# TensorE's first products of an expert placed behind the chain of comparisons, with a hinted jump to the rest

## The chip, the cores and the metric

The kernel runs on one core of one Trainium2 chip. The metric is the device time of one launch in microseconds (us), a median of runs. TensorE does the matrix products (in the profile PE for the products and PEld for the loading of their weights), VectorE is DVE, ScalarE is ACT, GpSimd is POOL, and SyncE (SP) issues the large transfers.

## What is computed

Two layers of an encoder trunk over 256 tokens of width 1024. The second layer ends in a mixture of experts, and the change touches that part alone:

```python
def moe_swiglu(h, w_router, b_router, w_gate_e, w_up_e, w_down_e):
    t = h.reshape(n, d)                                   # n = 256, d = 1024
    logits = (t @ w_router).astype(jnp.float32) + b_router.astype(jnp.float32)
    top_val, top_idx = lax.top_k(logits, TOP_K)           # 2 of 8 experts
    gates = jax.nn.softmax(top_val, axis=-1)
    ...
    def expert_block(args):
        xblk, e = args
        return swiglu(xblk, w_gate_e[e], w_up_e[e], w_down_e[e])   # width 3584
    ...
def swiglu(u, wg, wu, wd):
    return (jax.nn.silu(u @ wg) * (u @ wu)) @ wd
```

With the inputs of the measurement the eight experts get 3, 8, 109, 33, 131, 7, 166 and 55 rows.

## The kernel before

Every engine runs its own instruction stream. The experts are a loop over `turn` = 0 to 7 that each engine runs for itself. The routine `experts` (from line 668) writes it: the part `next` adds one to the counter and leaves after eight, `pick` loads the number of rows of this expert from `cnt`, and `tree` is a chain of compare-and-branch instructions that picks the body for 32, 64, 128, 160, 192 or 256 rows, the smallest that holds the count. So the bodies that run, in order, are those for **32, 32, 128, 64, 160, 32, 192 and 64** rows; this text calls them expert 0 to expert 7.

The bodies are written out in full, one behind the other, and are long on TensorE. An fp32 product (`mm` on F32 operands) is four instructions there, two weight loads and two matmuls, and an fp32r product is two. Counted in the built program, from the first instruction of `tree`, the bodies begin at 17 (128 rows), 1170 (32), 3531 (64), 4826 (160) and 7506 (192), and the last jump of the 160 body stands at 7504. A body begins with a hint (BRANCH_PREFETCH_HINT, written by `mark_branch_hint_location`) that names its own last instruction, a jump to `next`. The body for `first_variant`, 128 rows, stands straight behind `tree`. ScalarE and VectorE have the same structure with bodies of their own, and the change leaves theirs as they are.

An expert has 14 stages. A stage multiplies the rows by 256 columns of the gate and of the up weights (`gate_up`), applies silu and the product on ACT and DVE, turns the result (`turn`) and multiplies it by the down weights (`down`). Its weights are three units of 1 MB. SP fetches the units in order into 14 slots; a slot is free again when the stage that read it has counted up `gu_full` or `down_done`. For up to 64 rows `expert_whole` works on fp32 weights as they land. For 128 rows `expert_split`, for 160 and 192 rows `expert_wide`, ACT and DVE first split each unit into two fp32r parts (`conv_hi`, `conv_lo`); in `expert_wide` only stage 0 (`gate_up_whole`) uses the fp32 weights as they are, in two halves `h` of 16 products each. `xe_ready` says that the rows of the next expert have been copied by POOL.

[...]

## Time and profile before

| | us |
|---|---|
| median of three runs | 1688.39 |
| lowest and highest run | 1682.43, 1692.14 |
| the profiled execution | 1681.41 |
| its span, first to last instruction | 1679.6 |
| TensorE busy in the span | 1476.7 (88%) |
| the eight experts, from the first product of expert 0 | 680 to 1653 |

The profile says when each engine worked, what ended each idle stretch, and what the DMA queues moved. The windows list for each stretch the busy time and count of PE, PEld, DVE, ACT and POOL, then the granted share of TensorE's clock, the mean busy share of the DMA engines and what they moved.
### The profile page before, as it was taken

How to read it: one execution, taken by the hardware profiler on the slowest of the kernel's cores; microseconds unless marked ns; L12 is line 12 of the kernel's file. 1: busy time of each engine (PE TensorE's matmuls, PEld its weight loads, DVE VectorE, ACT ScalarE, POOL GpSimd, SP SyncE). 2: the span in 40 equal slices, each digit the busy share in tenths (PEclk: the TensorE clock that was granted, in tenths of full speed). 3: DMA queues.
4: the chain of work that ended last, by engine and by line, in shares of the span. 5: the costliest groups of instructions: out<-in, count | busy, mean ns of one | idle time of the engine just before them, and what ended most of it. 6: DMA issues, size and time to landing. Idle time of an engine off the chain costs nothing.

```text
span 1679.6 us, 30643 instructions
## 1 busy us (share of the span) xinstructions
PE 1476.7 (88%) x12410; PEld 1188.3 (71%) x12411; DVE 786.5 (47%) x1098; ACT 596.8 (36%) x795; POOL 69.4 (4%) x66
## 2 busy tenths in 40 slices
PE   5999899999999998765659999989996679999894
PEld 3878778999977876543548875689985468888452
DVE  2584565565556655100038851166761036665112
ACT  2445254444343433100036750146551035554101
POOL 0010100000010111000000000000000000000002
PEclk8999999999999999978789999999998889999998
DMA  9644567745333529899999999996667996555893
GB/s 361 238 159 172 202 225 293 282 176 197 141 116 109 223 76 386 352 425 423 425 425 426 406 384 425 424 391 279 244 270 312 425 424 249 224 226 225 329 425 148
DMA packets 69183, 488.89 MB, mean 291 GB/s; under 512 B 7744, under 2 KB 7776, under 8 KB 11168
## 3 DMA queue, kind: packets, MB, share of 16 engines
q1 hardware_dynamic: 66800, 479.94, 71.0%
q10 hardware_dynamic: 1648, 4.59, 0.8%
q8 instruction: 117, 1.92, 0.5%
q0 software_dynamic: 576, 2.10, 0.4%
q14 instruction: 42, 0.34, 0.1%
HBM read 482.66 MB, written 3.93 MB: 290 GB/s over the span
## 4 chain that ended last, share of the span: by engine, by line
PE 44%; DMA 10%; issue 4%; DVE 2%; ACT 1%; SPq 1%; POOL 1%; ACTq 0%; POOLq 0%; DVEq 0%
PE PG L1442 9%; DMA ring<-in_experts 8%; PE PG L1564 5%; PE PG L1499 4%; PE Y L1527 4%; PE Y L1454 4%; PE TRB L1499 4%; PE TRB L1505 3%; PE PG L1505 3%; PE Y L1595 2%; PE Y L1518 2%; DMA arena<-in_experts 2%; PE TRB L1428 2%; SPq L785 1%; PE Y L1251 1%
## 5 line engine op out<-in xcount | busy, mean ns | idle before, releaser
L2537 DVE COPY arena<-TRB 128x64 f32<-128x64 f32 (+1 forms) x70 | 17.6, 252 | 342.9 <-PE TRB L1428 342.9
L1442 PE MATMUL PG<-ring,mixT 128*32 128x128 f32 (+1 forms) x1920 | 115.3, 346 | 64.5 <-issue 59.9
L1647 ACT ACTIVATE rope<-PG 64x128 f32<-64x128 f32 (+2 forms) x84 | 27.3, 324 | 379.2 <-PE PG L1442 355.7
L1647 ACT ACTIVATE parts<-ring 128x2048 fp32r<-128x2048 f32 x82 | 153.7, 1902 | 9.4 <-PE PG L1564 5.1
L1442 PEld LDWEIGHTS PG<-ring,mixT 128*32 128x32 f32 (+1 forms) x1920 | 88.5, 137 | 94.5 <-issue 79.1
L944 PE MATMUL PG<-h_parts,parts 128*128 128x512 f32 x432 | 152.9, 394 | 1.4 <-DVE arena L2415 1.4
L1442 PE MATMUL PG<-arena,mixT 128*32 128x128 f32 (+1 forms) x1664 | 102.6, 355 | 41.8 <-issue 41.8
L1442 PEld LDWEIGHTS PG<-arena,mixT 128*32 128x32 f32 (+1 forms) x1664 | 79.7, 141 | 69.3 <-issue 55.7
L946 PE MATMUL PG<-h_parts,parts 128*128 128x256 f32 x432 | 121.8, 282 | 0.0
L2400 DVE TENSOR_TENSOR parts<-ring,parts 128x2048 fp32r<-128x2048 f32 x42 | 95.1, 2289 | 30.4 <-ACT parts L1647 30.4
L2521 DVE TENSOR_TENSOR ring_parts<-ring,parts 128x2048 fp32r<-128x2048 f32 x40 | 90.6, 2288 | 30.1 <-PE Y L1518 18.1
L2521 DVE TENSOR_TENSOR parts<-arena,parts 128x2048 fp32r<-128x2048 f32 x42 | 95.2, 2288 | 17.5 <-PE Y L1518 13.5
L944 PEld LDWEIGHTS PG<-h_parts,parts 128*128 128x128 f32 x432 | 81.2, 188 | 19.8 <-DVE arena L2415 1.6
L946 PEld LDWEIGHTS PG<-h_parts,parts 128*128 128x128 f32 x432 | 81.3, 188 | 0.0
L1647 ACT ACTIVATE parts<-arena 128x2048 fp32r<-128x2048 f32 x42 | 78.9, 1902 | 3.7 <-PE PG L1564 3.7
L911 PE MATMUL Y<-parts 128*128 128x256 f32 x224 | 63.5, 284 | 0.2 <-DVE parts L2424 0.2
L913 PE MATMUL Y<-parts 128*128 128x256 f32 x224 | 63.4, 283 | 0.0
L912 PE MATMUL Y<-parts 128*128 128x256 f32 x224 | 63.4, 283 | 0.0
L2090 DVE TENSOR_TENSOR ring_parts<-ring,ring_parts 128x2048 fp32r<-128x2048 f32 (+1 forms) x24 | 52.8, 2199 | 18.9 <-ACT ring_parts L1647 18.8
L2521 DVE TENSOR_TENSOR parts<-arena,scr_parts 128x2048 fp32r<-128x2048 f32 x21 | 48.2, 2293 | 26.4 <-ACT scr_parts L1647 26.4
L1454 PE MATMUL Y<-arena 128*32 128x256 f32 (+1 forms) x512 | 56.9, 445 | 3.0 <-issue 2.8
L1647 ACT ACTIVATE ring_parts<-ring 128x2048 fp32r<-128x2048 f32 (+1 forms) x24 | 43.8, 1837 | 41.3 <-PE Y L1251 30.1
(381 smaller groups left out, 2853.4 us busy)
## 6 DMA issues: line engine op xcount, KB each, us to landing
ring<-in_experts SPq DMA_DIRECT2D x168, 1024.0 KB, 14.0
arena<-in_experts SPq DMA_DIRECT2D x168, 1024.0 KB, 16.8
ring<-in_weights SPq DMA_DIRECT2D x116, 1024.0 KB, 6.5
ring<-in_weights SPq DMA_DIRECT2D x4, 512.0 KB, 5.2
ypairs<-hT ACTq DMA_DIRECT2D x3, 512.0 KB, 6.9
tok<-in_x SPq DMA_DIRECT2D x1, 1024.0 KB, 9.1
result<-scr SPq DMA_DIRECT2D x2, 512.0 KB, 2.6
ring<-in_weights SPq DMA_DIRECT2D x2, 432.0 KB, 6.0
```

The source lines that it names most:

```text
L911: mm(out_, w_hi[w][:, c], x[0], start=first, stop=False, skip_group_check=True)
L944: mm(PG[:, m, :].rearrange("p (i t) -> p i t", i=2), w_hi[d % SPLITS][:, c], h_parts[:, :, k, :], start=(k == 0), stop=False, skip_group_c ...
L946: last = mm(PG[:, m, 0:T], w_lo[d % SPLITS][:, c], h_hi[:, k, :], start=False, stop=(k == KD - 1), skip_group_check=True)
L1442: last = mm(bank[i * n:(i + 1) * n, 0:width], xe[:, k, 0:n], w[k // 4][:, k % 4, i * width:(i + 1) * width], start=(k == 0), stop=(k == KD ...
L1454: last = mm(o, actT[:, s % 2, f, 0:n], w[:, f, c:c + width], start=(s == 0 and f == 0), stop=(s == STAGES - 1 and f == 1))
L1499: last = mm(both, hi[:, k, i // 2, i % 2, :], h_parts[:, :, h * KD // 2 + k, 0:n], start=(h == 0 and k == 0), stop=False, skip_group_check ...
L1505: last = mm(bank[:, 0:n], lo[:, k, i // 2, i % 2, :], h_parts[:, 0, h * KD // 2 + k, 0:n], start=False, stop=(h == 1 and k == KD // 2 - 1) ...
L1527: last = mm(o, a[:, s % 2, f, :], w[:, f, c:c + width], start=(opens and s == 0 and f == 0), stop=(closes and s == STAGES - 1 and f == 1))
L1564: last = mm(bank, x[j][:, h * KD // 2 + k, :], w[:, k, :], start=(opens and k == 0), stop=(closes and k == KD // 2 - 1))
L1647: return nc.scalar.activation(out_, in_, func, **kw)
L2400: V.tensor_tensor(w_lo[d % SPLITS], ring[:, slot_of[slot_of_dense(d)], :, :].rearrange("p k c -> p (k c)"), w_hi[d % SPLITS].bitcast(F32), ...
L2521: V.tensor_tensor(w_lo_e[q % SLOTS_E], ring_e[q % SLOTS_E].rearrange("p k c -> p (k c)"), w_hi_e[q % HI].bitcast(F32), ALU.subtract).then_ ...
```

## The change

`experts` gets a parameter `heads`, which TensorE alone passes. For 64, 192 and 160 rows (`HEADS`) there is now a short body that stands straight behind `tree`: the wait for `xe_ready`, stage 0 of `gate_up` for 64 rows, or the first half of `gate_up_whole` for 160 and 192 rows, then a hinted jump to `rest_64`, `rest_192` or `rest_160`, which holds everything else. The body for 32 rows follows the heads and is whole. The bodies for 128 and 256 rows stay whole and stand farther back. The order of the products within an expert is the same as before.

```diff
+HEADS = (64, 192, 160)
...
-            for n in sorted(NVAR, key=lambda n: n != first_variant):
-                with nc.body(label(n), valid_engines=own):
+            if heads:
+                for n in HEADS:
+                    with nc.body(label(n), valid_engines=own):
+                        on = eng.mark_branch_hint_location()
+                        heads(eng.snap(turn, min_val=0, max_val=NE - 1), n)
+                        eng.br(label(f"rest_{n}")).branch_hint(on)
+            for n in sorted(NVAR, key=lambda n: n != (32 if heads else first_variant)):
+                parted = heads and n in HEADS
+                with nc.body(label(f"rest_{n}" if parted else n), valid_engines=own):
                     back = eng.mark_branch_hint_location()
+                    if heads and not parted:
+                        heads(eng.snap(turn, min_val=0, max_val=NE - 1), n)
                     emit(eng.snap(turn, min_val=0, max_val=NE - 1), n)
                     eng.br(label("next")).branch_hint(back)
...
-            def expert_whole(e, n):
+            def expert_whole(e, n, head):
...
-                for i in range(STAGES + 2):
+                if head:
+                    gate_up(0)
+                    return
+                for i in range(1, STAGES + 2):
...
-                gate_up_whole()
+                if head:
+                    gate_up_whole(0)
+                    return
+                gate_up_whole(1)
...
+                if head:
+                    gate_up(0)
+                    return
                 for s in range(STAGES + 1):
-                    if s < STAGES:
+                    if 0 < s < STAGES:
                         gate_up(s)
...
-            def expert(e, n):
+            def part(e, n, head):
+                (expert_whole if n < P else expert_split if n % P == 0 else expert_wide)(e, n, head)
+
+            def expert_head(e, n):
                 pe.wait_ge(xe_ready, e + 1)
-                (expert_whole if n < P else expert_split if n % P == 0 else expert_wide)(e, n)
-
-            experts(pe, "pe", expert)
+                part(e, n, True)
+
+            def expert_rest(e, n):
+                part(e, n, False)
+
+            experts(pe, "pe", expert_rest, first_variant=HEADS[0], heads=expert_head)
```

On TensorE this is what stands behind the load of the row count before the change. L691 and L693 are the comparisons, and L1564 belongs to the body for 128 rows:

```order
L684 UNCONDITIONAL_BRANCH
L691 COMPARE_AND_BRANCH x2
L693 COMPARE_AND_BRANCH x3
L696 BRANCH_PREFETCH_HINT
L697 ISA
L1468 ISA
L1580 ISA
L1564 MATMUL PG<-scr_parts,h_parts 128x512 x4
```

And this stands there in the changed kernel, whose lines are ten or more higher. L698 is a head's hint, L1452 are products of `gate_up` for 64 rows, L1495 those of `gate_up_whole`:

```order
L692 COMPARE_AND_BRANCH
L694 COMPARE_AND_BRANCH x4
L698 BRANCH_PREFETCH_HINT
L699 ISA
L1424 ISA
L1452 MATMUL PG<-ring,mixT 64x256 x16
L700 UNCONDITIONAL_BRANCH
...
L1495 MATMUL PG<-mixT,ring 128x160 x8
L1495 MATMUL TRB<-mixT,ring 128x160 x8
L700 UNCONDITIONAL_BRANCH
L704 BRANCH_PREFETCH_HINT
L706 ISA
L1424 ISA
L1452 MATMUL PG<-ring,mixT 32x128 x32
```

The 128 body has given its place to three heads of 16 products each (64 matmul and load instructions each), and the 32 body follows them. Counted from the first instruction of `tree` as before, the heads begin at 17, 87 and 156, the 32 body at 225, `rest_64` at 2587, the 128 body at 3816, `rest_160` at 4969 and `rest_192` at 7584.

The second place is the end of the 160 body on TensorE, before the change:

```order
L1468 REGISTER_ALU
L1535 REGISTER_ALU
L1527 MATMUL Y<-parts 128x512 x4
L1527 MATMUL Y<-parts,arow_parts 128x512 x4
L1527 MATMUL Y<-parts 128x512 x4
L698 UNCONDITIONAL_BRANCH
L696 BRANCH_PREFETCH_HINT
```

These products are the same in the changed kernel. What moved is the place of their jump in the stream: 7504 instructions behind `tree` before, 7582 now.

## Rows read from the trace of the kernel before

**Rows 1.** Page, part 4, chain that ended last: shares by engine.

```profile
PE 44%; DMA 10%; issue 4%; DVE 2%; ACT 1%; SPq 1%; POOL 1%; ACTq 0%; POOLq 0%; DVEq 0%
```

**Rows 2.** Windows: stretch, length, busy times, then PEclk, DMA share, GB/s.

```profile
758.00:864.00 106.00, 62.65 (x1165) 47.79 (x1156) 8.12 (x30) 5.80 (x17) 1.90 (x1) 0.81 1.01 424
871.00:997.00 126.00, 122.19 (x530) 98.83 (x531) 103.42 (x70) 86.44 (x71) 2.42 (x1) 0.97 1.00 411
998.00:1082.00 84.00, 83.13 (x616) 46.30 (x612) 10.77 (x29) 7.15 (x16) 1.90 (x1) 1.00 1.01 417
1082.00:1262.00 180.00, 173.67 (x1292) 155.74 (x1288) 118.83 (x100) 97.83 (x97) 1.90 (x1) 0.99 0.75 304
...
1567.00:1650.00 83.00, 83.00 (x606) 46.86 (x608) 10.08 (x28) 6.56 (x15) 0.00 (x0) 0.98 0.87 359
...
1268.00:1276.00 8.00, 3.94 (x76) 3.96 (x80) 0.00 (x0) 0.19 (x1) 0.00 (x0) 0.50 0.12 36
1300.00:1340.00 40.00, 26.22 (x480) 19.76 (x484) 2.60 (x10) 1.62 (x6) 0.00 (x0) 0.79 1.01 425
```

**Rows 3.** Timeline, PE, first products of experts 2 to 7, idle before.

```profile
871.42 3.52 PE L1564 MATMUL PG<-scr_parts,h_parts 128*128 128x512 f32 x8 [7.03 <-ACT scr_parts L1647]
...
997.75 7.13 PE L1442 MATMUL PG<-ring,mixT 128*64 128x256 f32 x64
...
1082.42 2.44 PE L1483 MATMUL PG<-mixT,ring 128*128 128x160 f32 x16
...
1272.07 6.22 PE L1442 MATMUL PG<-ring,mixT 128*32 128x128 f32 x128 [9.82 <-issue]
...
1359.16 4.55 PE L1483 MATMUL PG<-mixT,ring 128*128 128x192 f32 x16 [7.00 <-issue]
1363.54 2.76 PE L1483 MATMUL TRB<-mixT,ring 128*128 128x192 f32 x16
...
1566.99 9.00 PE L1442 MATMUL PG<-ring,mixT 128*64 128x256 f32 x64 [5.90 <-issue]
```

**Rows 4.** Jumps of the sequencer: ns least/median/most, first and last start.

```profile
L691 PEldq COMPARE_BRANCH  x1: 6457/6457/6457, 759.0 to 759.0; - x1
...
L698 PEldq COMPARE_BRANCH  x1: 1301/1301/1301, 863.5 to 863.5; - x1
...
L691 PEldq COMPARE_BRANCH  x2: 67/213/359, 995.8 to 995.9; - x2
...
L693 PEldq COMPARE_BRANCH  x3: 65/68/448, 1080.9 to 1081.2; - x3
...
L698 PEldq COMPARE_BRANCH  x1: 4015/4015/4015, 1261.2 to 1261.2; - x1
L691 PEldq COMPARE_BRANCH  x1: 5226/5226/5226, 1266.3 to 1266.3; - x1
...
L693 PEldq COMPARE_BRANCH  x2: 68/3168/6269, 1352.4 to 1352.5; - x2
...
L691 PEldq COMPARE_BRANCH  x2: 67/2626/5185, 1561.2 to 1561.3; - x2
```

**Rows 5.** Instruction packets: span, 868 to 870 us, 1266 to 1271 us.

```profile
q8 instruction: 117, 1.92, 0.5%
...
q8 instruction: 1, 0.02, 3.2%
...
q8 instruction: 2, 0.03, 4.3%
```

**Rows 6.** Timeline of ACT, PE and DVE at experts 2 to 4.

```profile
869.38 1.91 ACT L1647 ACTIVATE scr_parts<-ring 128x2048 fp32r<-128x2048 f32 x1
...
1072.09 3.67 PE L1442 MATMUL PG<-arena,mixT 128*64 128x256 f32 x32 [0.87 <-issue]
...
1089.05 2.34 PE L1483 MATMUL TRB<-mixT,ring 128*128 128x160 f32 x16
...
1095.08 0.49 DVE L2568 COPY rope<-PG 128x320 f32<-128x320 f32 x1
```

30 lines of the change are left out of this document (15 added, 15 removed).

## The prediction, made before the changed kernel ran

> **What bounds the kernel now.** I read the chain that ended last first: 44% of the span is TensorE, 10% transfers, and 4% "issue", time for which the profile names nothing [rows 1]. The windows by expert then say which expert is bound by what. Experts 0, 1 and 5 (32 rows) run at a DMA share of 1.01 and 424 to 425 GB/s while TensorE is busy for about 60% [rows 2]: the weights bound them. Experts 2, 4 and 7 are bound by TensorE (122 of 126 us, 174 of 180, 83 of 83), and so is expert 6, which is like expert 4 with more rows. Expert 3 is both: TensorE is busy for 83 of 84 us and the DMA share is 1.01.
>
> The timeline shows where TensorE stands still between experts [rows 3]: 7.03 us before expert 2, put down to ACT, nothing before experts 3 and 4, 9.82, 7.00 and 5.90 us before experts 5, 6 and 7, all "issue". The sequencer's records explain these three [rows 4]. A jump whose target is at hand takes 359 or 448 ns (to the bodies of experts 3 and 4, the longest record of each row). The others took 6457, 5226, 6269 and 5185 ns (experts 1, 5, 6, 7), and ahead of expert 5 the jump back to `next` took 4015 ns. Two packets of q8 fall in 1266 to 1271 us, around the 5226 ns [rows 5]. So I read a long jump as a fetch of code, price 5.2 to 6.5 us; the rows show no other work for which it could wait.
>
> From this come three rules. (1) A packet holds some 256 instructions: 117 packets for 24,821 loads and matmuls and some 1,200 instructions of the sequencer, with those fetched in vain. (2) On entering a block the next one in the stream is fetched: one packet in 868 to 870 us, 3 to 5 us after the tree was entered at 864.8, though no jump missed there [rows 4, 5]. When it is usable I take from two rows: 5.6 us after entry where DMA is full (at expert 1 it is 7.2 us from the tree's entry, 0.8 us ahead of the jump, to the end of the missed jump, which waited for two packets; less 1.5 for the second), and 4.0 where it is less so (the 4015 ns). (3) Several blocks stay: the jump of 359 ns went to code that the end of expert 1 had reached, 130 us earlier.
>
> The 4015 ns also tell where blocks are cut. A hint names the jump at a body's end, and only the 160 body had to wait so long for `next`; the fetch was late, so its last jump stands just behind a cut, by 1 to 25 instructions (the 12 products that close the body are 24). It is 7504 behind the tree, 29 blocks and 80. So a cut lies 55 to 79 behind the tree's start: in the 64 head, with the 192 and 160 heads and the first 86 to 110 instructions of the 32 body in the block behind the tree's.
>
> [...] The rows show a jump over nine blocks in 0.36 us. [...]
>
> **The parts.** All sums are changes of the profiled execution, 1681.41 us (span 1679.6 and 1.8 around it), 7 us below the median of 1688.39.
>
> *Experts 0 and 1*: their jump becomes shorter, but DMA bounds them, and expert 0 waits for POOL. 0.
>
> *Expert 2 (128 rows)*, which loses its place behind the tree. Today its first product waits until 871.42 for ACT's first conversion (869.38 and 1.91) [rows 3, 6]. Now the jump misses: the tree is entered at 864.8, or 0.9 earlier, since the 1301 ns of `next` fall to 0.4 where the 32 body's jump stands farther behind a cut. With 1.4 us for load and comparisons and 6.3 us for the miss it is 871.6 to 872.5, and 0.5 more to the first product: **0.8 us lost**, between 0 and 2.
>
> *Expert 3 (64 rows)*. Today there is no gap, since its body happens to be kept. Now the head is at hand, but `rest_64` is not. If the hint works as those of the bodies do, when the sequencer enters the block with the hinted jump, the fetch starts at about 997.5, some 50 instructions into the head, and takes 5.6 us: 1003.1. The head's products, half of the 7.13 us, end at 1001.3. **2.0 us lost**, with 0.2 for the start; 0.8 if the hint acts at once. Of both losses 0.87 us is covered: at 1072.09 TensorE waited that long for a unit of weights [rows 6], DMA being full. Together **1.9 us lost**. Without that cover it would be 2.8.
>
> *Expert 4 (160)*. Head at hand, 4.8 us of products in it (2.44 and 2.34), then the jump. A miss behind it leaves 2.9 us of gap, but `gate_up_whole` ended at 1091.4 and DVE got to its result only at 1095.08, behind conversions [rows 6]: 3.7 us of cover. **0**. If cover failed, 2.9.
>
> *Expert 5 (32)*. (a) The 160 body's jump moves to 7582 behind the tree, 79 to 103 behind a cut, so the hinted fetch is ready in time and 4.0 us become 0.3. (b) The 5.2 us jump goes to the block behind the tree, asked for on entry. Entry at 1261.5, block at 1266.4 (4.9, between full and idle DMA), first product at 1266.9 instead of 1272.07. (c) That block holds only about a hundred instructions of the body; the next, asked for at 1266.4, comes at 1270.4, behind which a quarter of stage 0 is left: it ends at 1271.8 instead of 1275.2. This counts, because the end of stage 0 frees slots, and DMA stood nearly idle until then (share 0.12 in 1268 to 1276, then 1.01 in 1300 to 1340) [rows 2]. **3.3 us gained**, 1.5 to 5.2.
>
> *Expert 6 (192)*. The tree is entered at 1351.35; its next block is usable at 1357.0, where the jump ended at 1358.8: 1.8 us earlier. The head lasts 7.3 us at the half clock (4.55 and 2.76) [rows 3], and a fetch asked for at its jump, 2 us in, is ready 7.7 us after its start. **1.4 us gained**, 0 to 1.9.
>
> *Expert 7 (64)*. Here the head stands in the tree's own block: it starts at 1562.3 instead of 1566.99 and runs for 4.5 us. The rest of it is there by 1564.4 (entry at 1560.4 and 4.0), and there the fetch of `rest_64` begins, 3.6 to 5.2 us. The rest begins at about 1569 instead of 1571.5. **2.5 us gained**, 1.7 to 4.7, and up to 1.9 more if the clock (half in this stretch: 9.00 us for what takes 7.13) recovers with the shorter stop.
>
> Extra comparisons and hints, five times 0.07 us and some 0.15, lie beside queued products. Sum: -0.8 -2.0 +0.87 +0 +3.3 +1.4 +2.5 = **5.3 us faster**, 0.3%: 1683.1.
>
> **The rivals.** *A head's hint fetches at once.* The bodies' hints don't tell, since theirs are blocks away from their jumps. Then expert 3 loses 0.8, and 6 and 7 gain 1.9 and 4.3: -0.7 +3.3 +1.9 +4.3 = 8.8, time 1679.6.
>
> *The block behind the tree doesn't help a jump that comes while it is under way*, because it is fetched a second time (1.5 us a packet). For it: I see no such jump in the trace. Then expert 5 gains 1.8, 6 nothing and 7 2.2, and it comes to 2.1: 1686.3.
>
> *The tree and heads are dropped before they are used again.* [...] Place: the end of the 128 body, whose last jump now stands about 24 to 48 behind a cut, with six blocks of its own since the tree. `next` waits 2.8 us, the block behind the tree comes 5.6 us later (1003.3), `rest_64` another 5.6: its products start at 1009.3 instead of 1001.3, 7.9 lost. Expert 4's head waits 3.5 us and then 2.9, less 3.7 of cover: 2.7. With 0.8 and 0.87 that is 10.5 lost against 7.2 gained: **3.3 us slower**, 1691.7. It decides once fewer than eight blocks are kept. Against it: the kept body of expert 3 had outlived six later fetches, so at least seven stay. [...]
>
> **How the numbers follow.** Chances: the forecast 0.40, the hint at once 0.28, the double fetch 0.15, the dropped blocks 0.17. The forecast is the likeliest, 1683.1. The best bounds of experts 5 to 7 and the clock make 12.6 us, 1675.8, and the last rival ends at 1691.7. The runs of before spread over 10 us, so I add one and two us: 1675 to 1694. A measurement tells about 0.5%, 8.4 us, from no change. Only the early hint with a clock gain passes that, or an upper end of the forecast: faster 0.25; slower 0.08, the last rival with its bounds; within 0.67.
>
> **What would show it.** The 4015 ns fall under 0.5 us, and the long comparisons at experts 6 and 7 shorten to 4.5 us and 0.1. A new long comparison stands before expert 2. The heads' jumps take 3 to 6 us if the hint is late and under 3 if it is early. PE's idle time before expert 5 falls from 9.8 to 5 us, with a second gap within its first stage. DMA's pause near 1270 shrinks by 3 us. Gaps of 1 to 3 us appear inside experts 3, 4, 6 and 7, behind 16 products. I am wrong if experts 3 and 4 begin with gaps over 3 us, if expert 5's earlier start doesn't bring its end forward, or if the cuts lie elsewhere than worked out.

## The result

| | before | after |
|---|---|---|
| median (20 runs each, same chip) | 1686.39 us | 1697.26 us |
| lowest and highest run | 1681.86, 1692.14 | 1690.39, 1702.81 |
| profiled execution | 1681.41 us | 1693.88 us |
| its span | 1679.6 us | 1692.1 us |

The ratio is 1.0067, with a 95% interval of 1.0054 to 1.0079: the change makes the kernel slower by two thirds of a per cent. The forecast was 1683.1 in a range of 1675 to 1694.

To see where it went, I took from both traces the time between the last product of one expert and the last of the next (their starts), so that each expert carries the idle time at its start. The loss lies in experts 3, 6 and 7, and a little in experts 0 and 1, which are 1.2 us longer together:

| us | 0 | 1 | 2 | 3 | 4 | 5 | 6 | 7 |
|---|---|---|---|---|---|---|---|---|
| before | 78.5 | 105.5 | 133.4 | 84.5 | 179.9 | 89.9 | 208.9 | 91.2 |
| after less before | -1.2 | +2.4 | 0.0 | +8.1 | +0.6 | -4.9 | +4.0 | +4.3 |

(Expert 0 is counted from its first product, which comes 0.6 us earlier after the change; the unrounded sum less 0.6 is the 12.5 us of the span.)

### The profile page after: what moved, and what is told of

Same layout as the page of the kernel before. It is cut to its first block, busy times and chain, and to the rows that moved or that the text cites. A ratio compares the mean times of both kernels' runs of the same rounds, so it can differ in the third digit from the quotient of the medians.

```text
span 1692.1 us, 30662 instructions
## 1 busy us (share of the span) xinstructions
PE 1492.1 (88%) x12410; PEld 1199.7 (71%) x12411; DVE 786.3 (46%) x1098; ACT 596.5 (35%) x795; POOL 69.4 (4%) x66
## 4 chain that ended last, share of the span: by engine, by line
PE 46%; DMA 9%; issue 4%; DVE 2%; ACT 1%; SPq 1%; POOL 0%; ACTq 0%; POOLq 0%; DVEq 0%
PE PG L1452 9%; DMA ring<-in_experts 7%; PE PG L1580 5%; PE PG L1512 4%; PE Y L1464 4%; PE Y L1540 4%; PE TRB L1512 4%; PE TRB L1518 3%; PE PG L1518 3%; PE Y L1611 2%; PE Y L1531 2%; DMA arena<-in_experts 2%; PE TRB L1438 2%; PE PG L1495 1%; PE Y L1261 1%
## 5 line engine op out<-in xcount | busy, mean ns | idle before, releaser
L1452 PE MATMUL PG<-ring,mixT 128*32 128x128 f32 (+1 forms) x1920 | 125.6, 361 | 65.1 <-issue 54.6
L1452 PEld LDWEIGHTS PG<-ring,mixT 128*32 128x32 f32 (+1 forms) x1920 | 95.6, 142 | 97.8 <-issue 82.2
L1452 PE MATMUL PG<-arena,mixT 128*32 128x128 f32 (+1 forms) x1664 | 102.6, 355 | 39.3 <-issue 39.3
L1452 PEld LDWEIGHTS PG<-arena,mixT 128*32 128x32 f32 (+1 forms) x1664 | 79.4, 140 | 66.2 <-issue 52.5
L1672 ACT ACTIVATE arena<-PG 128x512 f32<-128x512 f32 x29 | 17.4, 598 | 114.5 <-PE PG L956 105.6
```

Source lines behind the costliest of these rows:

```text
L1452: last = mm(bank[i * n:(i + 1) * n, 0:width], xe[:, k, 0:n], w[k // 4][:, k % 4, i * width:(i + 1) * width], start=(k == 0), stop=(k == KD ...
L1672: return nc.scalar.activation(out_, in_, func, **kw)
```

## The profile after

The timeline of PE at the starts of the experts answers [rows 3]. The value in brackets is the idle time ahead of the row.

```profile
872.07 3.78 PE L1580 MATMUL PG<-scr_parts,h_parts 128*128 128x512 f32 x8 [7.15 <-ACT scr_parts L1672]
...
998.27 3.67 PE L1452 MATMUL PG<-ring,mixT 128*64 128x256 f32 x32
1003.76 1.48 PE L1452 MATMUL PG<-ring,mixT 128*64 128x256 f32 x10 [1.81 <-issue]
1009.02 5.28 PE L1452 MATMUL PG<-ring,mixT 128*64 128x256 f32 x22 [3.78 <-issue]
...
1099.46 4.02 PE L1495 MATMUL PG<-mixT,ring 128*128 128x160 f32 x16 [3.85 <-issue]
...
1106.91 1.30 PE L1512 MATMUL PG<-h_parts,parts 128*128 128x320 f32 x7 [1.16 <-DVE rope L2593]
...
1274.74 2.35 PE L1452 MATMUL PG<-ring,mixT 128*32 128x128 f32 x38 [3.32 <-issue]
1279.38 5.24 PE L1452 MATMUL PG<-ring,mixT 128*32 128x128 f32 x90 [2.28 <-issue]
...
1361.56 5.21 PE L1495 MATMUL PG<-mixT,ring 128*128 128x192 f32 x16 [5.12 <-issue]
...
1372.64 4.54 PE L1495 MATMUL PG<-mixT,ring 128*128 128x192 f32 x16 [3.27 <-issue]
...
1570.53 3.76 PE L1452 MATMUL PG<-ring,mixT 128*64 128x256 f32 x32 [1.18 <-issue]
1577.44 2.26 PE L1452 MATMUL PG<-ring,mixT 128*64 128x256 f32 x10 [3.15 <-issue]
1583.41 5.11 PE L1452 MATMUL PG<-ring,mixT 128*64 128x256 f32 x22 [3.72 <-issue]
```

Experts 3 and 7 (64 rows) are to be read first. The head is 32 records of PE. Behind it comes the stop that I had counted on (1.81 and 3.15 us), but only ten records later, in the middle of the same stage, comes a second one of 3.78 and 3.72 us, which no part of the prediction had. Expert 6 now stands still twice, 5.12 and 3.27 us, instead of once for 7.00. And behind the second stop the same products take longer: 22 records in 5.28 us are 0.240 us each, where 32 took 3.67 us, 0.115 each, ahead of both. The windows show the clock over these stretches, with the granted share as the third value from the end; the first is that of the ten records between the two stops of expert 3:

```profile
1003.70:1005.20 1.50, 1.44 (x10) 0.88 (x11) 0.43 (x1) 0.14 (x1) 0.00 (x0) 1.00 0.97 388
...
1009.00:1014.50 5.50, 5.48 (x23) 3.73 (x23) 0.00 (x0) 0.10 (x1) 0.00 (x0) 0.50 0.41 171
...
1583.50:1588.50 5.00, 5.00 (x23) 3.42 (x22) 0.00 (x0) 0.00 (x0) 0.00 (x0) 0.53 0.01 3
```

It is still 1.00 behind the stop of 1.81 us, and 0.50 and 0.53 behind those of 3.78 and 3.72 us. Before, the granted clock was 1.00 in the first 7 us of expert 3 (998 to 1005 us; [rows 3], 7.13 us for 64 records, against 10.43 for the same now). So expert 3's 8.1 us are 5.6 of stops and 3.3 of products that took longer, less the 0.87 us for which it used to wait for weights later on. Most of the 3.3 is the clock: in the first experiment below the same 64 records, with one stop and a granted clock of 1.00, take 7.34 us.

The jumps of the sequencer answer [rows 4]. L700 is the jump from a head to its rest, L708 the jump back to `next`, L692 and L694 are the comparisons; columns are ns least/median/most, then the first and last start. That such a record on TensorE lasts until its sequencer goes on shows at expert 5 of the kernel before: the jump of 4015 ns starts at 1261.2 and the next record of the sequencer, the add in `next` (L679), at 1265.3; the comparison of 5226 ns starts at 1266.3 and the hint of the body that it leads to (L696) at 1271.6. Packets of q8 start in that comparison at 1266.8 and 1268.4.

```profile
L694 PEldq COMPARE_BRANCH  x4: 65/66/6228, 864.9 to 865.3; - x4
...
L700 PEldq COMPARE_BRANCH  x1: 3737/3737/3737, 999.6 to 999.6; - x1
...
L700 PEldq COMPARE_BRANCH  x1: 6164/6164/6164, 1093.0 to 1093.0; - x1
...
L708 PEldq COMPARE_BRANCH  x1: 319/319/319, 1270.4 to 1270.4; - x1
...
L692 PEldq COMPARE_BRANCH  x1: 2730/2730/2730, 1271.5 to 1271.5; - x1
...
L694 PEldq COMPARE_BRANCH  x2: 68/2366/4665, 1356.4 to 1356.5; - x2
...
L700 PEldq COMPARE_BRANCH  x1: 6151/6151/6151, 1366.2 to 1366.2; - x1
...
L700 PEldq COMPARE_BRANCH  x1: 5051/5051/5051, 1572.0 to 1572.0; - x1
```

`next` ahead of expert 5 fell from 4015 to 319 ns as forecast. But the heads' hinted jumps take 6164 and 6151 ns at experts 4 and 6, as long as a full miss (5.2 to 6.5 us in [rows 4]), and only expert 3's, of 3737 ns, is much shorter. The hint of expert 6's head ran 5.0 us ahead of its jump (1361.3 and 1366.2 us), and the jump was no shorter for it.

## The experiments

Two words are used below. A *cut* is the boundary between two blocks of 256 instructions, and a *slot* is the number of instructions between the last cut and an instruction. The 256 are my reading of [rows 5]; the profile gives the 16 KB of a packet and no count of instructions. I counted slots in each built program (without labels), with one fixed point from the first result: I took the 4015 ns of `next` to mean that the last jump of the 160 body stood close behind a cut (slot 31). The two stops inside a stage in the changed kernel fit both: 10 records, 20 instructions, and three ahead of them lie between the start of `rest_64` and the cut, and 38 records, 76 instructions, and four between the start of the 32 body and its cut. In the changed kernel the heads begin at slots 227, 40 and 108, the 32 body at 176, and `rest_64` at 233, 23 ahead of a cut. Each ratio is to the kernel before, run beside it. The code ahead of the experts is the same in every run, yet the first product of expert 0 comes at 679.4 to 690.1 us in the profiled executions. So the readings go by the time of each expert, as above, and a difference of a microsecond or so in one expert proves nothing by itself. A part is moved with a piece that is never run ahead of it:

```diff
+                    with nc.body(label(f"pad_{part}"), valid_engines=own):
+                        eng.addr_align(256, offset=PADS[part], max_nops=0)
+                        eng.br(label(...))
```

**The rests at cuts.** The changed kernel with `rest_64`, `rest_160` and `rest_192` just behind a cut each.

```diff
+PADS = {'rest_64': 0, 'rest_160': 0, 'rest_192': 0}
```

> The changed kernel with rest_64, rest_160 and rest_192 each moved to the first slot of a block of 256 instructions (a part that never runs pads in front of them); nothing else. Theory (near cut): in the changed kernel TensorE sends only 20 instructions of rest_64 and then stops 3.78 us (expert 3) and 3.72 us (expert 7) because rest_64 stands 20 instructions ahead of a cut and the next block was asked for only when this one was entered. With 256 instructions ahead both second stops vanish and the half clock behind them too: expert 3 gets 6 us shorter, expert 7 by 5 us, the whole 9 to 12 us faster than the changed kernel's 1692.1 span, so about 1681 to 1684, a ratio to the kernel before of 0.999 to 1.001. The first stops behind the heads (1.8, 3.9, 3.3, 3.2 us) stay. Rival (data): the second stops wait for a unit of weights or for ACT; then they stay at 3.7 us wherever the code stands, and the ratio stays at 1.007.

Measured: 1685.47 us, ratio to before 1.000 (0.998 to 1.002). PE, start of expert 3:

```profile
1001.03 3.67 PE L1468 MATMUL PG<-ring,mixT 128*64 128x256 f32 x32
1006.01 3.67 PE L1468 MATMUL PG<-ring,mixT 128*64 128x256 f32 x32 [1.31 <-issue]
```

The second stop is gone, and with it the half clock: the 32 records behind the head take 3.67 us, and the granted clock is 1.00 in 1006 to 1013 us. Expert 3 is 7.6 us shorter than in the changed kernel, expert 7 5.5. The order of the products is the same; the places of three parts made the difference between the changed kernel and one as fast as before. The changed kernel's other loss is still there: expert 6 takes 3.7 us longer than before.

**No hints in the heads.**

```diff
-                        on = eng.mark_branch_hint_location()
                         heads(eng.snap(turn, min_val=0, max_val=NE - 1), n)
-                        eng.br(label(f"rest_{n}")).branch_hint(on)
+                        eng.br(label(f"rest_{n}"))
```

> The changed kernel without the three hints in the heads; the jumps to the rests stay. Theory (a hint acts only when the block that holds its jump is entered later): the 160 and 192 heads have hint and jump in one block, so their jumps keep their 6.16 and 6.15 us; the 64 head's hint stands ahead of the cut, so at expert 3 the jump grows from 3.74 us to 5 to 6; at expert 7 it stays near 5 us. Total 0 to 2 us slower than the changed kernel, ratio to the kernel before 1.007 to 1.008. Rival (hints all help): all four jumps grow by 1 us or more, 5 us or more in all, ratio 1.010 or above. Rival (hints harm, a fetch in vain): it gets faster than the changed kernel by 1 us or more.

Measured: 1706.25 us, ratio 1.012 (1.009 to 1.014). It is 9 us slower than the changed kernel, where 0 to 2 were expected. The jump at expert 3, whose hint stands in one block and whose jump in the next, takes 7707 ns instead of 3737. At experts 4 and 6, with hint and jump in the same block, nothing changes (5982 and 6130 against 6164 and 6151). So the hint at expert 3 was worth 4 us, and those at experts 4 and 6 nothing. That they stand in the block of their jump isn't the reason by itself, as the run with the chain at a cut shows below. There was one more loss, which my theory had not: the jump to expert 4's head took 4551 ns (364 with the hints), with PE idle for 3.31 us. The four jumps out of the heads, the comparisons at expert 4, and PE behind them:

```profile
L699 PEldq COMPARE_BRANCH  x4: 5725/6056/7707, 1005.0 to 1583.6; - x4
...
L694 PEldq COMPARE_BRANCH  x3: 65/68/4551, 1097.9 to 1098.2; - x3
```

```profile
1103.01 4.63 PE L1494 MATMUL PG<-mixT,ring 128*128 128x160 f32 x16 [3.31 <-issue]
```

**The kernel before with its 160 body moved to a cut**, so that its last jump, which was 31 behind one, stands 120 behind it.

> The kernel before with its 160-row body alone moved to the first slot of a block, so that its last jump stands over 100 instructions behind a cut; no heads. Theory (a): the 4.02 us of the jump to next at the end of expert 4 fall to 0.3, expert 5 begins 3 to 4 us earlier, DMA restarts as much earlier, and the end comes 3 to 5 us earlier: ratio 0.997 to 0.998. Expert 4's own start, which ran on from the 64 body in the same block, becomes a missed jump of 6 us, of which 3.7 us are covered by ACT's and DVE's conversions: up to 2.5 us back, so 0.998 to 1.000. Rival: the 4.02 us had nothing to do with the place of the jump and stay; then the ratio is 1.000 to 1.002.

Measured: 1689.29 us, ratio 1.001 (0.9995 to 1.003). `next` ahead of expert 5 fell from 4015 to 321 ns and PE's idle time there from 9.82 to 5.37 us:

```profile
1280.45 1.94 PE L1458 MATMUL PG<-ring,mixT 128*32 128x128 f32 x32 [5.37 <-issue]
...
1579.30 3.25 PE L1458 MATMUL PG<-ring,mixT 128*64 128x256 f32 x14 [9.27 <-issue]
```

The jump to `next` behind expert 6:

```profile
L714 PEldq COMPARE_BRANCH  x1: 3562/3562/3562, 1569.0 to 1569.0; - x1
```

The gain was given back: the bodies behind had moved with it, the 192 body's last jump came to slot 14, and `next` took 3562 ns there, with 9.27 us idle ahead of expert 7 instead of 5.90. The 160 body was no longer in the block in which the 64 body ends and was missed too: the jump to it took 6055 ns, with 5.09 us idle ahead of expert 4. This confirms the reading of the 4015 ns in the prediction, twice, and shows that a place can't be mended without looking at every part behind it.

**The chain of comparisons at a cut**, heads and 32 body behind it, rests at cuts.

```diff
+PADS = {'next': 0, 'rest_64': 0, 'rest_160': 0, 'rest_192': 0}
```

> e1 with next, pick, tree and heads also moved to the first slot of a block, so that tree, three heads and the first instructions of the 32 body lie in one block. Theory (near cut): the stops in front of the heads go: the long comparisons of expert 5 (2.73 us) and 6 (4.67 us) fall to under 0.4, as does the wait inside the 64 head at expert 7; the 32 body gets its second stop after 15 products instead. The hint of the 64 head is now in one block with its jump, so at expert 3 that jump grows from 3.7 to 5.6 us. Against e1 experts 5 and 6 gain 2 to 4 us each, expert 3 loses 2: 3 to 5 us faster than e1, ratio to the kernel before 0.996 to 0.999. Rival (jumps out of the tree always cost a fetch): the long comparisons stay at 2.7 to 4.7 us and it equals e1.

Measured: 1690.62 us, ratio 1.002 (0.9995 to 1.003). The comparisons at experts 5 and 6 are short now, and expert 5 begins after 0.78 us. But the 32 body's last jump had come to slot 15, and `next` behind experts 0, 1 and 5 took up to 6021 ns; expert 2 starts with 13.44 us idle. All eight jumps to `next`, then PE:

```profile
L724 PEldq COMPARE_BRANCH  x8: 202/330/6021, 760.6 to 1657.2; - x8
```

```profile
880.27 3.77 PE L1596 MATMUL PG<-scr_parts,h_parts 128*128 128x512 f32 x8 [13.44 <-issue]
```

Here the hints and jumps of all three heads stand in one block, between slots 8 and 215, and the jump at expert 3 was expected to grow to 5.6 us. It took 3484 ns, and the one at expert 4 took 2985 ns, with a stop of 0.72 us behind the head instead of 3.85. Both jumps, and the packets of q8 from the hint of expert 4's head to the end of its jump (1091 to 1098 us):

```profile
L712 PEldq COMPARE_BRANCH  x2: 2985/3234/3484, 1008.9 to 1094.9; - x2
...
q8 instruction: 1, 0.02, 1.0%
```

The same packets in the changed kernel, 1089 to 1100 us:

```profile
q8 instruction: 2, 0.03, 1.1%
```

So the jump at expert 4 took half as long with hint and jump still in one block: a hint can act from there. At expert 4 here, and at expert 3 in this run, in the changed kernel and in the three others with hints and a head for 64 rows, one packet came between the hint and the end of the jump, and the rest was usable 5.9 to 6.4 us behind the hint, about as long as the jumps of the second group take. At expert 4 of the changed kernel and at expert 6 of both, two came, and the jump took 6.1 to 6.2 us. I read this as a fetch of the next block that was already under way in the second group when the hint ran, and not in the first; no run tests that alone. Expert 7, with 5051 and 4408 ns, lies between.

**`rest_64` at slot 200**, 56 ahead of a cut: between the changed kernel and the first experiment.

```diff
+PADS = {'rest_64': 200, '128': 0, 'rest_160': 0, 'rest_192': 0}
```

> The changed kernel, with rest_64 moved to 56 instructions ahead of a block cut (20 in the changed kernel, none behind the cut in the run that put it at one), and the bodies behind it each at a cut. Theory: the block behind the target is asked for when the target's block is entered, so the second stop is the fetch less the products that stand ahead of the cut. Expert 3: 26 records instead of 10 at 0.148 us each are 2.4 us more cover, 3.78 - 2.4 = 1.4 us of second stop. Expert 7: the same from 3.72 at 0.15 to 0.23 us a record, 0 to 1.3 us. The first stops (1.8 and 3.2) remain. Expert 3 takes 1.4 us more than with rest_64 at a cut, ratio 1.001 to before. Rival: the second stop is a cost of any taken jump into the middle of a block (a second packet asked for only when the first has been used up, or the half clock itself): then it stays at 3.5 to 4 us in both experts, or is gone as soon as the target is not the block's last part, ratio 1.003 or 1.000.

Measured: 1689.48 us, ratio 1.002 (1.0003 to 1.0036). PE at experts 3 and 7:

```profile
1008.40 3.21 PE L1468 MATMUL PG<-ring,mixT 128*64 128x256 f32 x26 [1.46 <-issue]
1013.82 1.08 PE L1468 MATMUL PG<-ring,mixT 128*64 128x256 f32 x6 [2.21 <-issue]
...
1578.47 4.89 PE L1468 MATMUL PG<-ring,mixT 128*64 128x256 f32 x26 [3.11 <-issue]
1583.91 1.08 PE L1468 MATMUL PG<-ring,mixT 128*64 128x256 f32 x6 [0.54 <-issue]
```

The second stop moved to where the cut now is, behind 26 records, and is shorter by what the 16 further records take: 2.21 us against 3.78 at expert 3 (1.4 expected), 0.54 against 3.72 at expert 7, where they ran at a granted clock of 0.64 (1.00 at expert 3). Three places (23, 56 and 256 instructions ahead of the cut) give 3.78, 2.21 and 0 us at expert 3, as it should be if the block behind a jump's target is asked for when the target's block is entered.

**A head for 64 rows alone.**

```diff
-HEADS = (64, 192, 160)
+HEADS = (64,)
+PADS = {'rest_64': 0}
```

> The changed kernel with a head for 64 rows alone; 160 and 192 rows are whole bodies again, rest_64 stands at a cut, and the 160 body's last jump 196 behind one. Theory: the head and rest of 192 rows cost expert 6 4.0 us (two stops of 5.12 and 3.27 us at the half clock instead of one of 7.00), which come back; expert 4's body is missed at its start, with its first product 5 to 6 us late, of which up to 3.7 are covered by ACT and DVE, so it loses 1 to 2; expert 5 keeps its 4.9; expert 7 as with rest_64 at a cut (+3.5 to before), expert 3 +1.5, expert 2 +0.65. Sum against before: +0.65 +1.5 +1.5 -4.9 +0 +3.5 = +2.3, ratio 1.001. Rival: expert 6 ends late because of what stands ahead of it (its later start in the span) and not because of its head; then its loss of 4 us stays, ratio 1.004.

Measured: 1687.06 us, ratio 1.000 (0.998 to 1.002). Expert 6 was at +2.5 us to before instead of +4.0, but 2.2 of it is `next`, 2573 ns since the 32 body's last jump now stands at slot 96 (319 at slot 232); the comparison took 6412 ns. So the head's own 4 us came back. Expert 7 gained 3.0 against before, not the loss of 3.5 that I had carried over from the changed kernel: with the rest at a cut the head for 64 rows is worth having there. Expert 3 lost 0.9. Expert 4 lost nothing, since the jump to its body took 364 ns where a miss was expected. But expert 2 lost 5.4, with `next` at 4724 ns.

**The kernel before with the 32 body first and no heads**, the chain at a cut.

```diff
+ORDER = (32, 64, 160, 192, 128, 256)
+PADS = {'next': 0, '128': 0}
...
-            experts(pe, "pe", expert)
+            experts(pe, "pe", expert, first_variant=32)
```

> The kernel before with its bodies in another order and place, and no heads at all: the chain of comparisons at a cut, the body for 32 rows straight behind it in the same block, then 64, 160, 192, 128. Theory: what the change gains at expert 5 comes from the 32 body's standing behind the chain, and the heads only cost. Expert 5: next and the long comparison both go, its first product 9 us earlier than before (9.82 us idle become 1), no stop inside; expert 2 loses 0.65 (its body is now missed); experts 3 (body kept in the block where the 32 body ends), 4 (in the block where the 64 body ends), 6 and 7 as before. Sum -8.4 us, ratio 0.995, 0.993 to 0.997. Rival: expert 5 is bound by DMA and by the slots that expert 4 frees; then its earlier start is waited away in its stages, its end moves by 2 to 4 us only, ratio 0.998 to 0.999.

Measured: 1692.12 us, ratio 1.0035 (1.002 to 1.005): slower where 0.995 was expected. The mechanism that I had named held: expert 5 ends 8.9 us earlier. But `next` behind the 32 body, at slot 65, took 5831, 5403 and 4122 ns, and experts 2 and 6 began with 11.95 and 11.19 us idle instead of 7.03 and 7.00. I had taken 52 slots as enough from `rest_160` in the runs above (its last jump there, `next` at 319 and 335 ns), whose products are longer: the records of its last 52 instructions begin 4.8 us ahead of the jump (first experiment, 1261.6 and 1266.4 us), those of the 65 here 1.4 us ahead (760.7 and 762.1). So I count the time between the cut and the jump, and not the instructions.

**The same with everything ahead of the 128 body moved by 135**, so that the 32 body's last jump is at slot 200.

```diff
-PADS = {'next': 0, '128': 0}
+PADS = {'next': 135, '128': 0}
```

> The run with the 32 body first, all of it moved by 135 instructions, so that the last jump of the 32 body stands 200 instructions behind a cut instead of 65, and its start 111 ahead of one instead of 246. Theory: the hint at a body's start acts when the block with the jump is entered, and 65 instructions of the 32 body last less than a fetch, which is why next took 5831, 5403 and 4122 ns there. At 200 it takes under 0.5 us behind experts 0, 1 and 5; experts 2 and 6 start 4 to 5 us earlier than in that run, expert 5 loses 0 to 1 to a stop inside its stage 0 where the block behind its start is late. Ratio 0.996 to 0.998. Rival: next is late behind the 32 body because ten blocks have been read since it was used, and no place of the jump helps; then the three jumps stay over 4 us and the ratio 1.003.

Measured: 1679.33 us, ratio 0.996 (0.994 to 0.998). The six jumps to `next` behind experts 0 to 5, first in the run with slot 65:

```profile
L715 PEldq COMPARE_BRANCH  x6: 206/2227/5831, 762.1 to 1354.5; - x6
```

and then with slot 200:

```profile
L715 PEldq COMPARE_BRANCH  x6: 206/330/987, 756.7 to 1344.4; - x6
```

Same instructions, other addresses: 12.8 us of median apart, 0.75% by the ratios. It also beats the kernel before.

**32 first, with a head for 192 rows in the block in which the 32 body ends.**

```diff
+HEADS = (192,)
+PADS = {'next': 0, '160': 224, 'rest_192': 64, '128': 0}
```

> The run with the 32 body first, and a head for 192 rows straight behind the end of the 32 body, in the block where that body ends, with its rest at slot 64 of a block of its own; 64 rows stand whole behind this head, 160 in the block where 64 ends. Theory: at expert 6 the head's block is at hand, since expert 5 ended in it, so the 7.00 us of idle become 1; its hinted jump stands in the same block as the hint, so it still takes 6 us, with a stop of 3.3 us behind the 16 products. Expert 6 gains 2.5 to 4 us over the run without this head, expert 3 is unchanged: ratio 0.992 to 0.994. Rival: a head costs more than its stop, through the half clock that the stop brings on, as experts 6 and 7 of the changed kernel show: then expert 6 gains nothing over the run without it, ratio 0.995.

Measured: 1689.97 us, ratio 1.003 (1.001 to 1.004), where 0.993 was expected. It shares the late `next` (5849 ns ahead of expert 6), and with it its head at hand is worth little. PE at expert 6:

```profile
1366.19 5.48 PE L1512 MATMUL PG<-mixT,ring 128*128 128x192 f32 x16 [6.75 <-issue]
...
1377.24 3.18 PE L1512 MATMUL PG<-mixT,ring 128*128 128x192 f32 x13 [2.83 <-issue]
```

Against the run without this head (11.19 us idle once) the sum of stops is 9.6 us, but expert 6 is 0.3 us longer. The gain went to the clock behind the second stop: the 32 records there take 7.35 us at a granted clock of 0.76 (1377.2 to 1384.4 us), and without this head 5.52 us at 1.00 (1374.6 to 1380 us). Here the rival was right in its mechanism. The jump out of the head, in one block with its hint, took 6134 ns, as long as a full miss. Expert 4, moved to slot 224, 32 ahead of a cut, has a stop of 2.83 us behind 14 records, between the 3.78 and 2.21 us for 23 and 56 ahead of one.

**The choice behind each body.** From the kernel before: no body of TensorE jumps back; `next`, `pick` and `tree` are repeated behind each, and the bodies stand in the order 128, 64, 160, 32, 192.

```diff
+ORDER = (128, 64, 160, 32, 192, 256)
...
+            def choose(k, first):
...
             for i, n in enumerate(order):
                 own_choice = name == "pe" and n < 256
                 with nc.body(label(n), valid_engines=own):
...
                     emit(eng.snap(turn, min_val=0, max_val=NE - 1), n)
                     if own_choice:
                         eng.br(label(f"next{n}"))
...
                 if own_choice:
                     choose(n, order[i + 1])
```

> The kernel before (no heads) with a copy of next, pick and tree behind the end of each of TensorE's bodies, so that no body jumps back, and the bodies in the order 128, 64, 160, 32, 192, 256, so that experts 3 to 6 run into the body that stands next in the stream. Theory: what is lost between experts is fetches behind taken jumps, and a block that follows in the stream is there in time. Then experts 3, 4, 5 and 6 begin without a long comparison (under 0.5 us each), expert 5 gains 8.9 us as in the run with the 32 body first, expert 6 5.5 to 7.0 (its 7.00 us of idle become 1), expert 2 loses 0 to 0.7 (its jump stays long but comes 1.3 us earlier), expert 7 stays as before (6 us, jump long). Sum -14 us, ratio 0.990 to 0.993. Rival: the time that expert 6 needs at its start is that of the rows copied by POOL or of the weights, and the fetch only hides it; then expert 6 gains under 2 us, ratio 0.995.

Measured: 1672.40 us, ratio 0.992 (0.990 to 0.995). PE at the starts of experts 5, 6 and 7:

```profile
1268.57 3.70 PE L1456 MATMUL PG<-ring,mixT 128*32 128x128 f32 x128 [0.61 <-issue]
1279.89 0.76 PE L1442 MATMUL TRB<-con,rope 64*128 64x128 f32 x2 [7.62 <-DVE rope L2529]
...
1350.59 2.87 PE L1497 MATMUL PG<-mixT,ring 128*128 128x192 f32 x16 [1.33 <-DMA ring<-in_experts]
...
1557.88 9.67 PE L1456 MATMUL PG<-ring,mixT 128*64 128x256 f32 x64 [3.56 <-issue]
```

9.82 and 7.00 us of idle time are 0.61 and 1.33, and expert 5 ends 8.6 us earlier, expert 6 3.9 (5.5 expected: a wait one stage on grew from 1.3 to 3.2 us). The end of expert 5 came forward although its first stage now waits 7.62 us for DVE.

**The choice behind each body, order as before.**

```diff
-ORDER = (128, 64, 160, 32, 192, 256)
+ORDER = (128, 32, 64, 160, 192, 256)
```

> As the run with the choice behind each body (ratio 0.992), but with the bodies in the order of the kernel before: 128, 32, 64, 160, 192. Theory: most of that run's gain is from bodies that stand behind the one that runs ahead of them; what the missing jump back gives alone is the 4.0 us of next ahead of expert 5. Experts 3 (64 rows, behind the block in which expert 1 ended) and 4 begin without a long jump; experts 5, 6 and 7 start with one of 5 to 6.5 us as before, expert 5 with 5 us less idle time than its 9.8. Ratio 0.997 to 0.998. Rival: the gain is from the missing jump back and the missing hints; then experts 6 and 7 start early too, or the ratio stays at 0.992 to 0.994.

Measured: 1684.02 us, ratio 0.999 (0.997 to 1.001). Expert 5 gained 6.5 us, experts 6 and 7 began with long comparisons as expected. But expert 3, whose jump was short in the kernel before (359 ns), took 6092 ns and lost 6.4 us.

**The same, moved so that the 128 body lies in five blocks instead of six.**

```diff
+                    eng.addr_align(256, offset=250, max_nops=0)
```

> The run with the choice behind each body and the order kept (0.999), in which expert 3's jump to the 64 body took 6092 ns, moved by 31 instructions so that the 128 body begins just behind a cut and lies in five blocks instead of six. Theory: eight blocks are kept. The block with the start of the 64 body is followed by eight packets there before expert 3 needs it, and by six in the kernel before (jump 359 ns); here it is seven, so the jump takes under 0.5 us, expert 3 starts 4.5 us earlier and the ratio is 0.996. Rival: what drops the block is not the count but the missing hints (the next block is then fetched in the place of the hinted one); then the jump still takes 6 us, ratio 0.999.

Measured: 1675.39 us, ratio 0.994 (0.992 to 0.996). The comparisons ahead of expert 3, the last of them with the jump, in the run ahead of this one:

```profile
L698 PEldq COMPARE_BRANCH  x5: 65/65/6092, 999.3 to 999.8; - x5
```

and in this one:

```profile
L703 PEldq COMPARE_BRANCH  x5: 65/65/228, 996.4 to 996.9; - x5
```

Four kernels now tell how many blocks are kept. Counted from the packet that brought the block of the 64 body's start (as the end of the 32 body, experts before) to the jump of expert 3:

| kernel | packets of q8 in between | jump |
|---|---|---|
| before | 6 (852 to 995 us) | 359 ns |
| 32 first | 7 (862 to 1005) | 377 ns |
| choice, 128 in five blocks | 7 (851 to 998) | 228 ns |
| choice, 128 in six blocks | 8 (858 to 999) | 6092 ns |

With seven later ones the block is there (377 and 228 ns), with eight it is gone (6092 ns): in these four kernels TensorE keeps eight blocks.

**A second 64 body behind the 192 body**, on TensorE alone.

```diff
-ORDER = (128, 64, 160, 32, 192, 256)
+ORDER = ((128, 128), (64, 64), (160, 160), (32, 32), (192, 192), ("64b", 64), (256, 256))
```

> As the run with the choice behind each body, and a second copy of the body for 64 rows behind the 192 body, to which that body's own choice leads. Theory: the last long jump on a path that TensorE bounds goes; expert 7 begins 5.5 us earlier (5.90 us of idle become 0.3 to 1) and without the half clock that follows a stop (9.00 us for its first products become 7.1). Ratio lower by 0.003 to 0.005 than that run, 0.986 to 0.989. Rival: expert 7 waits for its weights or rows as soon as it comes earlier (DMA share 0.87 there): then it gains under 2 us, 0.001.

Measured: 1678.48 us, ratio 0.995 (0.993 to 0.997). Expert 7 begins after 0.61 us, and gained nothing; 0.986 to 0.989 was expected. The median is 6 us above that of the run without the second body, the time of all experts in the profiled execution 2.8 us, of which expert 7 has 2.4; why the medians are so far apart I can't say. The timeline of PE there:

```profile
1553.26 7.13 PE L1459 MATMUL PG<-ring,mixT 128*64 128x256 f32 x64 [0.61 <-issue]
1565.13 1.22 PE L1445 MATMUL TRB<-con,rope 64*128 64x128 f32 x4 [4.74 <-DVE rope L2532]
```

and of ACT:

```profile
1562.87 1.28 ACT L1664 ACT_TABLE_LOAD   x1 [8.97 <-issue]
```

TensorE waits for DVE, DVE for ACT, and ACT for "issue": its last comparison starts at 1557.57 and the first instruction of its body at 1562.65. In the last run below, where that body stands next in ACT's stream, the same two are 0.4 us apart (1562.49 and 1562.85): ACT misses its own code here. The record of that comparison lasts only 50 ns: on ACT the wait stands behind the record of the jump and not, as on TensorE, in it. The stop on TensorE had covered that one.

**The choice behind the bodies of ACT and DVE too.**

```diff
-                own_choice = name == "pe" and n < 256
+                own_choice = n < 256
```

> The run with TensorE's choice behind each body (0.992), with the same done for the bodies of ACT and DVE: a copy of the choice behind each, order 128, 64, 160, 32, 192, 256. Theory: what is left of a removed stop on TensorE at expert 5 is waited away because ACT and DVE miss their own code there (3.8 and 4.1 us between the comparison and the first instruction of the body in that run, then 7.62 us of TensorE idle behind DVE). Expert 5 runs into the next body on all three engines, so the 7.62 us fall to 1 to 3; as the weights bound expert 5 (share 1.01) only 2 to 4 us of it reach its end. Expert 7 is missed on all three as before. Ratio 0.990. Rival: TensorE waits there for the weights of expert 5, which are late whatever ACT does; then DMA or DVE ends the same wait at the same time and the ratio stays at 0.992.

Measured: 1671.24 us, ratio 0.992 (0.989 to 0.994). PE behind the first products of expert 5, then ACT:

```profile
1277.91 0.46 PE L1442 MATMUL TRB<-con,rope 64*128 64x128 f32 x2 [3.82 <-DVE rope L2529]
```

```profile
1275.59 1.28 ACT L1661 ACT_TABLE_LOAD   x1 [4.39 <-issue]
```

PE's wait of 7.62 us fell to 3.82 and ACT's of 8.40 to 4.39, so the cause was right; but expert 5 ends no earlier (-8.3 us to before, -8.6 without it). Behind its first stage the weights bound it (the DMA share is 1.01 in 1282 to 1351 us), and a wait that they cover is worth nothing. I had put 2 to 4 us on it.

**The same with the second 64 body on all three engines.**

> The run with a second body for 64 rows behind the 192 body (0.995, where expert 7 began 4 us earlier and then stood 4.74 us behind DVE and ACT), now with the choice and the second body on ACT and DVE as well. Theory: the 4.74 us are ACT's fetch of its own 64 body (its first instruction came 5.0 us behind its comparison); with it gone expert 7 ends 4 to 5 us earlier than in that run, expert 5 2 to 4. Ratio 0.987 to 0.990. Rival: the second stop is late weights or copies; then expert 7 gains under 1 us and the ratio is 0.992 to 0.995.

Measured: 1667.98 us, ratio 0.988 (0.986 to 0.990), the fastest of this study and 1.2% faster than the kernel before. PE at expert 7, then ACT:

```profile
1558.11 7.13 PE L1459 MATMUL PG<-ring,mixT 128*64 128x256 f32 x64 [0.57 <-issue]
1565.17 0.71 PE L1445 MATMUL TRB<-con,rope 64*128 64x128 f32 x4
```

```profile
1563.01 0.38 ACT L1664 ACTIVATE rope<-PG 64x256 f32<-64x256 f32 x1 [4.22 <-issue]
```

The 4.74 us are gone, ACT's idle time is 4.22 instead of 8.97, and expert 7 is 6.8 us shorter than before, where the second body on TensorE alone made it 0.8 us longer. One more thing has changed: the ACT_TABLE_LOAD of 1.28 us with which expert 7 began on ACT is not there, so up to 1.3 us of this is not the fetch's. The order of bodies in this run follows the order in which this input visits them; another routing would visit other neighbours, and that wasn't tried.

## Why the prediction was wrong

The reading of what bounds the kernel held: long jumps are fetches (in the changed kernel too, each TensorE jump of over 2 us has one or two packets of q8 in it), a block is some 256 instructions, the last jump of the 160 body stood just behind a cut, the next block is asked for on entry, kept blocks stay. The jump at expert 3 that it took as proof of this went even farther than it says: the 64 body stands 3531 behind the tree, some fourteen blocks and not nine. The sum failed at three of its terms.

- **Expert 3 (-2.0 in the sum, +0.87 cover; measured -8.1).** The failed step is "the fetch takes 5.6 us: 1003.1 ... 2.0 us lost". The rest was usable at 1003.4, 0.3 us from what was worked out. But the sum asked only when the target is at hand, not how much of its block is left. `rest_64` stands 23 instructions ahead of a cut, so rule 2 of the prediction itself brought a second fetch, 3.78 us. The numbers for it stood in the section on the change (`rest_64` at 2587, cuts every 256; by the prediction's own place of the cut it is 28 to 52 ahead of one): it was an omission. To this came 3.3 us of longer products, most of it clock, and the 0.87 us of cover were there as counted. With the rest at a cut the term measures 0.4 us lost.
- **Expert 7 (+2.5; measured -4.3).** The same omission, 3.72 us, plus the clock. The start did come earlier, by 4.7 us as worked out. The 64 records took 11.1 us without the stops instead of the 9.0 of before (granted clock 0.63 behind the first stop and 0.53 behind the second, 0.79 in those 9 us before), where I had priced a chance of a clock gain and none of a loss.
- **Expert 6 (+1.4; measured -4.0).** Two steps failed. "A fetch asked for at its jump, 2 us in": the sequencer reached that jump at 1366.2 us, 5.0 behind the hint and only 0.4 ahead of the 17th of the head's 32 PE records (1366.6). And behind the two stops (5.12 and 3.27 us) the clock was lower than behind the one of 7.00: 0.70 in 1361.5 to 1369.5 and 0.63 in 1372.6 to 1377.2 us, against 0.75 in 1359 to 1366.3 and 1.00 in 1366.3 to 1372.8 before. The stage's 64 records took 15.3 us instead of 12.8, and the 13.6 us from its first product to the next stage's became 19.5.
- **Expert 5 (+3.3 in 1.5 to 5.2; measured +4.9).** Right in each part: `next` 319 ns, the comparison 2730 instead of 5226, a stop inside stage 0, and the earlier end of that stage counted. The stop came behind 38 records: 80 instructions of the body stand ahead of the cut, where the prediction had 86 to 110. Its counts take in labels, and the jump of the 160 body is 31 behind a cut, not 1 to 25.
- **Expert 4 (0; measured -0.6).** The gap behind the head was 3.85 us (2.9 expected), and the wait for DVE fell from 4.81 to 1.16: the cover of 3.7 held.
- **Expert 2 (-0.8, between 0 and 2; measured 0.0).** The new long comparison came, with 6228 ns, but TensorE stood idle only 0.12 us longer (7.15 instead of 7.03), beside ACT's conversion. The first product is 0.65 us later because expert 1 ended 0.5 later.
- **Experts 0 and 1 (0; measured -1.2).** No run tells where this comes from; it is small enough to be chance.

Of the rivals, dropped blocks gave nearly the right size (1691.7) by the wrong mechanism. `next` behind expert 2 took 206 ns and the heads were at hand at experts 3 and 4. By the table of four kernels above, eight blocks are kept. The early hint's sizes did not come: expert 3 stopped for 1.81 us behind its head, and experts 6 and 7 for 3.27 and 3.15. As a mechanism it holds in part: the hint did nothing at experts 4 and 6, but at expert 3 the rest was usable a whole fetch behind it, 6.4 us. The rival that ended on the slow side had the right sign and got a chance of 0.17; no rival asked for the place of the target.

What stays open: why the jump to expert 4's head became long without the heads' hints. The packets suggest that where a block holds a hinted jump, its target is fetched in the place of the next block (no packet in 964 to 998 us in the kernel before, whose 128 body ends with a hinted jump, one in 968 to 998 where it ends without), so that fewer blocks are pushed out. The single packet at expert 4 of the run with the chain at a cut fits this. That is read from counts, not tested alone. Open is also when the heads' hints act and when not.

## What to carry to other kernels

Treat a taken jump in a long program as a load: ask where its target is fetched (a miss took 5.2 to 6.5 us here before the change), how many instructions of the target's block are left, and what runs meanwhile. A target 23 instructions ahead of a cut cost a second stop of 3.78 us at expert 3, and behind a cut by 14, 31 and 65 instructions the jump to `next` took 3562, 4015 and up to 5831 ns, although it was hinted at its body's start. In this kernel it was better to lay code out so that it runs on into the next body (ratio 0.992) than to hide a jump (1.0067), since every part moved moves the cuts of all parts behind it. When one engine's stop is removed, look for the same stop on the engines that it waits for (4.74 us behind DVE and ACT at expert 7), and count nothing where transfers bound the stretch (at a DMA share of 1.01 a wait shorter by 3.8 us brought expert 5's end no further forward).

## What the runs showed of the hardware that I had not expected

- In four kernels TensorE kept eight blocks: seven later packets left a block at hand (228 to 377 ns for the jump), an eighth did not (6092 ns).
- The hint at a body's start, blocks ahead of its jump, seems to act no earlier than about the block of that jump: with the jump 65 slots behind a cut in a body of 32 rows, `next` took 4.1 to 5.8 us, with 200 slots 0.3 to 1.0. A hint in the block of its jump did nothing in the changed kernel (6151 ns with, 6130 without) while in the run with the chain at a cut two such jumps took only 2985 and 3484 ns.
- A jump that landed near the end of a block brought a second stop: 3.78, 2.21 and 0 us for 23, 56 and 256 instructions ahead of the cut, at expert 3.
- Behind the stop of 1.81 us at expert 3 the granted clock was 1.00, behind that of 3.78 us it was 0.50 for 5.5 us; with the start of the stage this cost most of 3.3 us on top of 5.6 us of stops.
- ACT missed its code like TensorE: 5.1 us between its comparison and the first instruction of its body, 0.4 where the body stands next in its stream.
